# The residual reload of two feed-forward stages: one 4 MB transfer, or eight pieces beside eight output blocks

## The chip, the cores and the metric

The kernel runs on one core of one Trainium2 chip, in one launch. The metric is the device time of that launch in microseconds. A core has a matrix engine (PE), a vector engine (DVE), an activation engine (ACT), GpSimd (POOL) and a queue engine (SP), each with its own instruction stream; they wait for each other on semaphores. Transfers run on 16 DMA engines. Here SP issues the loads of weights (queue q1 in the profile), POOL those of the residual and of the hidden rows (queue q0).

## The reference, cut to what matters

Two blocks of layers on a sequence of 1024 tokens of 1024 channels, in float32. The second block has two feed-forward stages (FFN) with a mixer between them, and each of the three stages adds its normalised result to the stream `x`:

```python
def second_block(x, ...):
    h = rms_norm(x, ffn1_pre_g)
    x = x + 0.5 * rms_norm(swiglu(h, ffn1_w_in, ffn1_w_out), ffn1_post_g)
    h = rms_norm(x, mix_pre_g)
    ...                                   # attention and S5 state space, side by side
    x = x + rms_norm(mixed, mix_post_g)
    h = rms_norm(x, ffn2_pre_g)
    x = x + 0.5 * rms_norm(swiglu(h, ffn2_w_in, ffn2_w_out), ffn2_post_g)
    return x
```

The `x` on the right of each sum is the residual. [...]

## The kernel before, in words

All products are made of float32 operands split in a high and a low part, three products for one. A *block* is one 128-channel column of an output, made from a 128x1024 piece of weights. Its life: SP loads it into `WS` (`load_block`, line 324, two slots in turn); ACT copies it as the high part into `WH` (`split_hi`, line 333), when the block two before has been multiplied; DVE subtracts to get the low part `WL` (`split_lo`, line 340); that frees the `WS` slot, and SP loads the block two further on; PE multiplies (`block_products`, line 376); DVE takes the result out of PSUM. So each engine's order is fixed by hand, and a late load is seen first by ACT, then DVE, then PE.

The second product of an FFN is made in three parts (8, 6 and 8 rows of 128). The third is the *tail*: first the 8 blocks m = 0 to 7 of the first half of the tokens (h = 0), then the same 8 of the second (h = 1), each 24 products of 128x512. In the tail u (u = 1 for the first FFN, 2 for the mixer, 3 for the second FFN), per block: `tail_vector` adds PSUM into `ACC` (line 2205) and then splits the weights of block m + 2, `tail_scalar` copies the high part of block m + 2 and squares the finished column (`post_square`, line 2097), `tail_pool` adds that square to a running sum (`post_sum`, line 2103). At h = 1 the same engines also finish h = 0: `post_apply` scales the column and adds the residual (lines 2129 and 2133), from m = 2 on. The h = 1 half is finished in the next stage's first blocks (`head_vector`) for u = 1, and for u = 3 on PE, where `out_residual` turns the upper half of the residual (line 3601), from m = 2 on.

The residual lies in DRAM as `XRES` (`x_residual` in the profile) and comes back to `RL_X` for u = 1 and 3, which takes the place of `XL`, that is free once the second part's last block has been multiplied. `reload_pool` (line 2299) waits on POOL for that, and issues one transfer of 4 MB. The mixer's tail does it otherwise: `tail_pool` calls `reload_piece` there (line 2305) in the blocks m = 1 to 4 of either half, eight transfers of 512 KB, into `RL_A` and `RL_B`. The semaphore `RESID` counts the reloads (16 for each transfer), and `S5TOE`, a counter of the S5 mixer, is used again for the upper half of the mixer's.

Of the kernel before, what the change touches and what calls it, by code (L numbers as in the profile page):

```python
# [23 lines left out]
KT = D // P  # L24
# [22 lines left out]
S5_T = 8  # L47
# [31 lines left out]
B_MIX = B_FFN1 + FFN_BLOCKS  # L79
# [10 lines left out]
B_END = B_FFN2 + FFN_BLOCKS  # L90
# [54 lines left out]
def _build(nc, ctx, ins, out):  # L145
# [127 lines left out]
    RL_X = at("RL_X", 96, [P, KT, SEQ])  # L273
    RL_A = at("RL_A", 140, [P, 4, SEQ])
    RL_B = at("RL_B", 156, [P, 4, SEQ])
# [22 lines left out]
    XRES = nc.dram_tensor("x_residual", [KT, P, SEQ], F32, kind="Internal").ap()  # L298
# [1765 lines left out]
    FT_TAIL = B_FFN1 + FFN_BLOCKS - 2 * KT  # L2064
    PRE_G = ("f1_pre", "m_pre", "f2_pre")
    POST_G = (None, "f1_post", "m_post", "f2_post")
    RES_COUNT = (0, 16, 80, 96)

    def residual(u, k):
        return RL_X[:, k] if u != 2 else (RL_A[:, k] if k < 4 else RL_B[:, k - 4])  # L2070
# [49 lines left out]
    def post_apply(dve, u, h, rows):  # L2120
        if rows and rows[0] == 0:
            dve.wait_ge(P_RSTD, 2 * (u - 1) + h + 1)
            if h == 0:
                dve.wait_ge(RESID, RES_COUNT[u])
            elif u == 2:
                dve.wait_ge(S5TOE, 16 * S5_T + 64)
        for k in rows:
            x = ACC[:, k, half(h)]
            nc.vector.scalar_tensor_tensor(x, x, vec(POST_G[u], k), RPS[u][:, h], ALU.mult, ALU.mult).then_inc(P_SCALED, 1)  # L2129
        for k in rows:  # L2130
            dve.wait_ge(P_SCALED, place(u - 1, h, k))
            x = ACC[:, k, half(h)]
            nc.vector.tensor_tensor(x, x, residual(u, k)[:, half(h)], ALU.add).then_inc(XRDY, 1)
# [102 lines left out]
    def tail_pool(pool, u):  # L2236
        for h in range(2):
            for m in range(KT):
                if m:
                    post_sum(pool, u, h, m)  # L2240
                if u == 2 and 1 <= m < 5:
                    reload_piece(pool, h, m - 1)
                if h == 1:
                    for k in TAIL_HIGH.get(m, ()) if u < 3 else ():
                        pre_sum(pool, u, 0, k)
        spill_pool(pool, u, 0)
# [49 lines left out]
            pool.wait_ge(XRDY, place(u - 1, h, KT - 1))  # L2296
        pool.dma_start(XRES.rearrange("k p t -> p k t")[:, :, half(h)], ACC[:, :, half(h)]).then_inc(SPILLED, 16)

    def reload_pool(pool, u, b_last):
        pool.wait_ge(SPILLED, 32 * u)  # L2300
        for b in (b_last - 1, b_last):
            pool.wait_ge(BLOCK_DONE[b % 2], times(b))
        pool.dma_start(RL_X[:], XRES.rearrange("k p t -> p k t")).then_inc(RESID, 16)

    def reload_piece(pool, h, n):
        dst, k = (RL_A, RL_B)[n // 2], 2 * (n % 2)
        src = XRES[2 * n:2 * n + 2, :, half(h)].rearrange("k p t -> p k t")
        pool.dma_start(dst[:, k:k + 2, half(h)], src).then_inc(RESID if h == 0 else S5TOE, 16)

# [1043 lines left out]
    def s5_scalar(act, st):  # L3353
        hi = lambda b: split_hi(act, b, cols=cols_of(b))

        def keep_att(m):
            b = att_block(m)
            act.wait_ge(BLOCK_DONE[b % 2], times(b))
            if m == 1:
                act.wait_ge(S5_PRODUCTS, S5STATE[1])  # L3360
            nc.scalar.activation(PARTS[m][:], PS[b % 2][:, half(0)], ACT.Copy).then_inc(PS_READ[b % 2], 1)

        def copy_kernel(k):
            act.wait_ge(S5_PRODUCTS, S5KER[k])
            nc.scalar.activation(s5_half(K0S, k)[0:16], s5_bank(k)[0:16], ACT.Copy).then_inc(S5_COPIES, 1)

        def copy_y(k):
            for r in range(2):
                act.wait_ge(S5_PRODUCTS, S5Yp + 2 * k + r + 1)
                dst = UG[:, 8 * k:8 * k + 8].rearrange("p (q r) m -> p q r m", r=2)[:, :, r]  # L3370
                nc.scalar.activation(dst, s5_bank(r)[:, 4 * (k % 2):4 * (k % 2) + 4], ACT.Copy).then_inc(S5_COPIES, 1)

        def gelu(k):
            act.wait_ge(S5YL[k], YL_BASE[k] + 16)
            nc.scalar.activation(by_place(ZF[:, k]), S5Y[:, k].rearrange("p (j n) -> p n j", j=S5_T), ACT.Gelu_apprx_tanh).then_inc(S5ACT, 1)
            act.wait_ge(S5ACT, 2 * k + 1)
            if k == 0:
                act.wait_ge(S5_RESULTS, 4)
            if k == 3:
                act.wait_ge(S5_PRODUCTS, S5Yp + 8)  # L3380
            nc.scalar.activation(ZH[:, k], ZF[:, k], ACT.Copy).then_inc(S5ACT, 1)

        for k in range(4):
            act.wait_ge(S5_PRODUCTS, S5GT + k + 1)
            nc.scalar.activation(GIN[:, 4 * k:4 * k + 4].rearrange("p q r m -> p (q r m)"), PAB[k % 2][:], ACT.Copy).then_inc(S5_COPIES, 1)
        hi(att_block(2))
        keep_att(0)
        hi(att_block(3))
        copy_kernel(0)
        copy_kernel(1)  # L3390
        hi(att_block(4))
        keep_att(1)
        keep_att(2)
        hi(att_block(5))
        hi(att_block(6))
        copy_kernel(2)
        copy_kernel(3)
        keep_att(3)
        keep_att(4)
        copy_y(0)  # L3400
        copy_y(1)
        hi(B_GLU)
        keep_att(5)
        act.wait_ge(S5TOE, 16 * S5_T)
        gelu(0)
        copy_y(2)
        gelu(1)
        keep_att(6)
        copy_y(3)
        gelu(2)  # L3410
        hi(B_GLU + 1)
        gelu(3)

        def gate(m):
            b = B_GLU + m
            act.wait_ge(BLOCK_DONE[b % 2], times(b))
            if m >= 2:
                act.wait_ge(S5GATED, XLD_END + m - 1)
            nc.scalar.activation(T[m % 2][:], PS[b % 2][:], ACT.Sigmoid, bias=vec("bglu", m)).then_inc(PS_READ[b % 2], 1)
            hi(b + 2)  # L3420

        def gated_high(m):
            act.wait_ge(S5GATED, XLD_END + m + 1)
            nc.scalar.activation(XH[:, m], ZF[:, m], ACT.Copy).then_inc(S5ACT, 1)

        gate(0)
        for m in range(1, 4):
            gate(m)
            gated_high(m - 1)
        gated_high(3)  # L3430
        keep_att(7)
        hi(B_MIXOUT + 1)
        tail_scalar(act, st, 2)
# [76 lines left out]
    def s5_y(pe, k):  # L3510
# [1 line left out]
            pe.wait_ge(S5_COPIES, S5KC + 4)  # L3512
            pe.wait_ge(UD, 16 + 16 * S5_T)
        if k == 2:
            pe.wait_ge(S5TOE, 16 * S5_T)
        if k >= 2:
            pe.wait_ge(S5_COPIES, S5YC + 2 * k - 2)
        pe.wait_ge(S5_RESULTS, k + 1)
# [73 lines left out]

    def out_residual(pe, i):
        if i == 0:
            pe.wait_ge(RESID, RES_COUNT[3])
        if i == 1:
            pe.wait_ge(P_RSTD, 5)
        if i >= 2:
            pe.wait_ge(FCOPY, i - 1)
        for k in range(KT):  # L3600
            last = nc.tensor.transpose(PAB[1 - i % 2][:, k * P:(k + 1) * P], RL_X[:, k, (4 + i) * P:(5 + i) * P], IDENT[:])
        last.then_inc(FTURN, 1)
# [74 lines left out]
    def _(pool):  # L3677
# [5 lines left out]
        ssd_pool(pool)  # L3683
        ln2_pool(pool)
        quads_pool(pool, 0, B_FFN1)
        reload_pool(pool, 1, B_MIX - 2 * KT - 1)
        tail_pool(pool, 1)
        head_pool(pool, 1)
        s5_parameter_loads(pool)
# [5 lines left out]
        tail_pool(pool, 2)  # L3695
        head_pool(pool, 2)
        quads_pool(pool, 1, B_FFN2)
        reload_pool(pool, 3, B_END - 2 * KT - 1)
        out_gains(pool)
        tail_pool(pool, 3)  # L3700

# [63 lines left out]
```

## Time and profile before

| | us |
|---|---|
| median of 3 runs | 3339.81 (3339.54 to 3341.7) |
| the profiled execution | 3333.25 |
| its span (first to last instruction) | 3331.6 |
| PE busy | 3189.6 (96%) |
| DVE busy | 2047.3 (61%) |
| ACT busy | 1301.0 (39%) |
| POOL busy | 376.5 (11%) |
| mean granted PE clock | 0.986 |

The profile is of one execution, shorter than the median of the runs beside it. Times of events are counted from the start of its span. "Idle before" is the time for which an engine stood still just ahead of an instruction, with what released it. Successive products overlap on PE: one of 128x512 is shown 0.39 us long at full clock, and the next begins 0.23 us after it. "PEclk" is the clock that PE was granted, as a share of full speed.

### The profile page before, as it was taken

To read this page: it belongs to the slowest core of one execution; us is meant where nothing else is said; L and a number is where in the kernel's file an instruction comes from. 1 tells how busy PE (TensorE), PEld (TensorE's weight loads), DVE (VectorE), ACT (ScalarE), POOL (GpSimd) and SP (SyncE) were. 2 spreads that over 40 slices of the span, in tenths; PEclk is the share of its full clock that TensorE was granted. 3 is DMA by queue.
4 is the path that set the end of the run, shared out by engine and by line. 5 is a ranking of instruction groups with operands and counts; after the bars stand their busy time and mean duration, and the time that the engine had idled before them with its cause. 6 is when DMAs were issued, how large, how long until landed. Compare 5 with 4: busy or idle time off the path is not lost.

```text
span 3331.6 us, 39702 instructions
## 1 busy us (share of the span) xinstructions
PE 3189.6 (96%) x15786; PEld 2508.4 (75%) x15786; DVE 2047.3 (61%) x2783; ACT 1301.0 (39%) x1924; POOL 376.5 (11%) x412
## 2 busy tenths in 40 slices
PE   8998999999999999899999999998989899999998
PEld 7765677878787786578888877786667678888877
DVE  5545567664554646777777556686665777676334
ACT  2664435452525343742323224314434442323223
POOL 1010000110302010200000003140012300000012
PEclk9999999999999999899999999999999999999999
DMA  6210112222514132332224243422154432225232
GB/s 158 49 42 6 54 51 59 76 83 73 103 51 126 45 94 71 98 112 81 76 96 157 94 141 93 122 70 86 19 119 131 136 98 76 101 76 171 81 115 101
DMA packets 362981, 299.37 MB, mean 90 GB/s; under 512 B 54832, under 2 KB 324624, under 8 KB 362512
## 3 DMA queue, kind: packets, MB, share of 16 engines
q1 hardware_dynamic: 340400, 215.16, 22.6%
q0 software_dynamic: 22400, 81.69, 7.6%
q8 instruction: 126, 2.06, 0.3%
q14 instruction: 55, 0.45, 0.0%
HBM read 240.32 MB, written 52.95 MB: 88 GB/s over the span
## 4 chain that ended last, share of the span: by engine, by line
PE 78%; DVE 10%; ACT 5%; issue 4%; DMA 2%; SPq 0%; POOL 0%; ACTq 0%; DVEq 0%; POOLq 0%
PE PS L376 45%; PE PS L2483 13%; PE PA L2483 7%; PE PS L887 2%; DVE WL L340 1%; PE PA L898 1%; PE PB L1798 1%; DVE XL L2152 1%; DMA WS<-in_ffn_w_out_dram 1%; PE PB L910 1%; PE PA L416 1%; DVE ACC L2129 1%; PE PB L1146 1%; PE PB L1804 1%; PE PA L1780 1%
## 5 line engine op out<-in xcount | busy, mean ns | idle before, releaser
L376 PE MATMUL PS<-XH,WH 128*128 128x512 f32 x1744 | 592.9, 405 | 31.8 <-DVE XL L2152 19.0
L333 ACT ACTIVATE WH<-WS 128x1024 fp32r<-128x1024 f32 (+1 forms) x251 | 242.2, 968 | 846.6 <-PE PS L376 794.1
L376 PE MATMUL PS<-XH,WL 128*128 128x512 f32 x1680 | 554.4, 391 | 0.0
L376 PE MATMUL PS<-XL,WH 128*128 128x512 f32 x1648 | 543.0, 392 | 0.0
L376 PEld LDWEIGHTS PS<-XH,WH 128*128 128x128 f32 x1744 | 326.8, 189 | 127.3 <-DVE XL L2152 27.3
L340 DVE TENSOR_TENSOR WL<-WS,WH 128x1024 fp32r<-128x1024 f32 (+1 forms) x251 | 284.6, 1134 | 167.3 <-ACT WH L333 153.8
L376 PEld LDWEIGHTS PS<-XH,WL 128*128 128x128 f32 x1680 | 317.2, 189 | 67.7
L376 PEld LDWEIGHTS PS<-XL,WH 128*128 128x128 f32 x1648 | 311.3, 189 | 66.2 <-issue 2.2
L376 PE MATMUL PS<-TQH,WH 128*128 128x512 f32 x448 | 162.2, 397 | 7.9 <-DVE WL L340 7.9
L376 PE MATMUL PS<-TQH,WL 128*128 128x512 f32 x448 | 160.5, 393 | 0.0
L376 PE MATMUL PS<-TQL,WH 128*128 128x512 f32 x448 | 160.5, 393 | 0.0
L2483 PE MATMUL PS<-XH,PH 128*128 128x512 f32 x360 | 140.2, 390 | 1.7 <-issue 1.7
L2483 PE MATMUL PS<-XH,PL 128*128 128x512 f32 x360 | 140.1, 389 | 0.0
L2483 PE MATMUL PS<-XL,PH 128*128 128x512 f32 x360 | 140.1, 389 | 0.0
L1911 ACT ACTIVATE DEC<-DEC,NCS 128x128 f32<-128x128 f32 x256 | 78.3, 388 | 98.0 <-POOL DEC L2027 97.9
L1932 DVE TENSOR_TENSOR DEC<-DEC,PB 128x1024 f32<-128x1024 f32 x32 | 39.1, 1222 | 125.6 <-ACT DEC L1911 102.8
L2483 PE MATMUL PS<-TQH,PH 128*128 128x512 f32 x288 | 112.5, 390 | 1.8 <-DVE U3S L2729 1.0
L2483 PE MATMUL PS<-TQL,PH 128*128 128x512 f32 x288 | 112.1, 389 | 0.0
L2483 PE MATMUL PS<-TQH,PL 128*128 128x512 f32 x288 | 112.1, 389 | 0.0
L2483 PE MATMUL PA<-TQH,PH 128*128 128x512 f32 x288 | 112.0, 389 | 0.0
L2483 PE MATMUL PA<-TQL,PH 128*128 128x512 f32 x288 | 112.0, 389 | 0.0
L2483 PE MATMUL PA<-TQH,PL 128*128 128x512 f32 x288 | 112.0, 389 | 0.0
(685 smaller groups left out, 6230.6 us busy)
## 6 DMA issues: line engine op xcount, KB each, us to landing
RAW<-in_ffn_w_in_dram SPq DMA_DIRECT2D x36, 1024.0 KB, 5.2
WS<-in_ffn_w_out_dram SPq DMA_DIRECT2D x48, 512.0 KB, 4.1
WS<-in_ssd_w_in_dram SPq DMA_DIRECT2D x40, 512.0 KB, 3.9
DEC<-ssd_decay_sums SPq DMA_DIRECT2D x32, 512.0 KB, 4.8
WS<-in_ffn_w_in_dram SPq DMA_DIRECT2D x32, 512.0 KB, 4.0
CDX<-ssd_decays SPq DMA_DIRECT2D x56, 256.0 KB, 3.7
TQF<-ffn_hidden POOLq DMA_DIRECT2D x14, 1024.0 KB, 8.2
x_residual<-ACC POOLq DMA_DIRECT2D x6, 2048.0 KB, 7.7
```

The costliest lines, as they stand in the source:

```text
L333: nc.scalar.activation(WH[:, s, 0:cols], WS[:, s, 0:cols], ACT.Copy).then_inc(W_HI[s], 1)
L340: nc.vector.tensor_tensor(WL[:, s, 0:cols], WS[:, s, 0:cols], WH[:, s, 0:cols].bitcast(F32), ALU.subtract).then_inc(W_LO[s], 1)
L376: last = nc.tensor.matmul(PS[s][0:width, c], w[:, s, k * width:(k + 1) * width], x[:, k - x0, c], start=(k == 0 and j == 0), stop=(k == kt ...
L416: last = nc.tensor.matmul(PA[:, h * HALF:(h + 1) * HALF], ONES[:], bufs[k % 2][:, h * HALF:(h + 1) * HALF], start=(k == 0), stop=(k == kts ...
L887: last = nc.tensor.matmul(PS[s][:, a + c * P:a + (c + m) * P], self.queries(p, s)[:, qb * P:(qb + 1) * P], self.keys(p, s)[:, c * P:(c + m ...
L898: last = nc.tensor.transpose(PA[:, s * HALF + (kb - 4 * c) * P:s * HALF + (kb - 4 * c + 1) * P], self.probs(u, s)[:, kb * P:(kb + 1) * P], ...
L910: last = nc.tensor.matmul(PB[HD * s:HD * s + HD, HALF + (qb % 4) * P:HALF + (qb % 4 + 1) * P], self.values(p, s, kb), PT[u % 2][:, s, kb * ...
L1146: last = nc.tensor.matmul(bank, WUQ[:, c // 2, kt], Y[:, 4 + kt, h], start=(kt == 0), stop=(kt == 1))
L1780: nc.tensor.matmul(PA[:, half(c % 2)], BTOK[:, c], XDD[c % 2][:], start=True, stop=True).then_inc(SST, 1)
L1911: last = nc.scalar.activation(d, d, ACT.Exp, bias=NCS[:, c, k:k + 1])
L1932: v.tensor_tensor(DEC[n % 2][:], DEC[n % 2][:], PB[:, 0:P].unsqueeze(1).broadcast_to([P, HPG, P]), ALU.mult).then_inc(SMR, 1)
L2483: last = nc.tensor.matmul(bank, w[:, j, k * P:(k + 1) * P], x[:, k], start=(j in (A11, S2, S1) and k == 0 and t == 0), stop=(k == 3 and t ...
```

## The change: what it does

`reload_pool` becomes `reload_ready`: POOL waits as before, and issues nothing. `tail_pool` issues the pieces for u = 1 and 3 as well: at h = 0, after the sum of block m, piece m (channels 2(m mod 4) and 2(m mod 4) + 1 of 128 each, token half m // 4), so eight pieces of 512 KB in each of the two tails, all in h = 0. Pieces of the lower token half count on `RESID`, those of the upper on `S5TOE`; all waits on these two are moved to the new counts, and two readers of the upper half wait on `S5TOE`: `post_apply` at h = 1 for u = 1, and `out_residual`.

```diff
-    RES_COUNT = (0, 16, 80, 96)
+    RES_COUNT = (0, 64, 128, 192)
+    RES_HIGH = (0, 64, 64 + 16 * S5_T + 64, 64 + 16 * S5_T + 128)
...
             if h == 0:
                 dve.wait_ge(RESID, RES_COUNT[u])
-            elif u == 2:
-                dve.wait_ge(S5TOE, 16 * S5_T + 64)
+            elif u < 3:
+                dve.wait_ge(S5TOE, RES_HIGH[u])
...
                 if u == 2 and 1 <= m < 5:
-                    reload_piece(pool, h, m - 1)
+                    reload_piece(pool, u, h, m - 1)
+                if u != 2 and h == 0:
+                    reload_piece(pool, u, m // 4, m % 4)
...
-    def reload_pool(pool, u, b_last):
+    def reload_ready(pool, u, b_last):
         pool.wait_ge(SPILLED, 32 * u)
         for b in (b_last - 1, b_last):
             pool.wait_ge(BLOCK_DONE[b % 2], times(b))
-        pool.dma_start(RL_X[:], XRES.rearrange("k p t -> p k t")).then_inc(RESID, 16)
-
-    def reload_piece(pool, h, n):
-        dst, k = (RL_A, RL_B)[n // 2], 2 * (n % 2)
+
+    def reload_piece(pool, u, h, n):
+        dst, k = ((RL_A, RL_B)[n // 2], 2 * (n % 2)) if u == 2 else (RL_X, 2 * n)
         src = XRES[2 * n:2 * n + 2, :, half(h)].rearrange("k p t -> p k t")
         pool.dma_start(dst[:, k:k + 2, half(h)], src).then_inc(RESID if h == 0 else S5TOE, 16)
...
-        act.wait_ge(S5TOE, 16 * S5_T)
+        act.wait_ge(S5TOE, 64 + 16 * S5_T)
...
         if k == 2:
-            pe.wait_ge(S5TOE, 16 * S5_T)
+            pe.wait_ge(S5TOE, 64 + 16 * S5_T)
...
     def out_residual(pe, i):
         if i == 0:
-            pe.wait_ge(RESID, RES_COUNT[3])
+            pe.wait_ge(S5TOE, RES_HIGH[3])
...
-        reload_pool(pool, 1, B_MIX - 2 * KT - 1)
+        reload_ready(pool, 1, B_MIX - 2 * KT - 1)
         tail_pool(pool, 1)
...
-        reload_pool(pool, 3, B_END - 2 * KT - 1)
+        reload_ready(pool, 3, B_END - 2 * KT - 1)
         out_gains(pool)
         tail_pool(pool, 3)
```

## Rows read from the trace of the kernel before

**Rows 1.** The page's chain that ended last, by engine.

```profile
PE 78%; DVE 10%; ACT 5%; issue 4%; DMA 2%; SPq 0%; POOL 0%; ACTq 0%; DVEq 0%; POOLq 0%
```

**Rows 2.** The waits of the whole span: us in total, times, longest.

```profile
ACT WH L333 <- DMA WS<-in_ffn_w_out_dram: 20.2, 2, 10.1
```

**Rows 3.** The chain in order of time, first FFN's tail: start, us, what.

```profile
1974.67 14.76 DMA WS<-in_ffn_w_out_dram
...
1989.45 1.06 ACT WH L333
...
1990.54 1.24 DVE WL L340
```

**Rows 4.** The chain in order of time, second FFN's tail.

```profile
3214.84 14.75 DMA WS<-in_ffn_w_out_dram
```

**Rows 5.** PE in order of time, first FFN's tail: start, us, idle before.

```profile
1991.82 0.53 PE L376 MATMUL PS<-TQH,WH 128*128 128x512 f32 x1 [3.27 <-DVE WL L340]
```

**Rows 6.** PE in order of time, second FFN's tail.

```profile
3231.98 0.79 PE L376 MATMUL PS<-TQH,WH 128*128 128x512 f32 x1 [3.27 <-DVE WL L340]
```

**Rows 7.** DVE in order of time, first FFN's tail: results of blocks 1, 3 and 4.

```profile
1983.14 0.69 DVE L2205 TENSOR_TENSOR ACC<-ACC,PS 128x512 f32<-128x512 f32 x1 [3.06 <-PE PS L376]
...
1999.22 0.69 DVE L2205 TENSOR_TENSOR ACC<-ACC,PS 128x512 f32<-128x512 f32 x1 [5.23 <-PE PS L376]
...
2004.66 0.69 DVE L2205 TENSOR_TENSOR ACC<-ACC,PS 128x512 f32<-128x512 f32 x1 [3.06 <-PE PS L376]
```

**Rows 8.** DVE in order of time, second FFN's tail: results of blocks 1 and 3.

```profile
3223.32 0.69 DVE L2205 TENSOR_TENSOR ACC<-ACC,PS 128x512 f32<-128x512 f32 x1 [3.06 <-PE PS L376]
...
3240.59 0.69 DVE L2205 TENSOR_TENSOR ACC<-ACC,PS 128x512 f32<-128x512 f32 x1 [6.44 <-PE PS L376]
```

**Rows 9.** Busy time by stretch: us; PE, PEld, DVE, ACT, POOL; PEclk, DMA share, GB/s.

```profile
1991.80:1999.10 7.30, 7.28 (x25) 5.83 (x26) 2.19 (x2) 0.80 (x2) 3.12 (x2) 0.77 0.48 144
...
3232.00:3240.50 8.50, 8.50 (x25) 6.75 (x26) 2.15 (x2) 0.77 (x2) 3.08 (x2) 0.65 0.45 123
```

**Rows 10.** DMA from 1960 to 2000: packets and MB of each queue; KB each, us to landing.

```profile
q0 software_dynamic: 1040, 4.19, 28.1%
q1 hardware_dynamic: 6112, 3.08, 26.8%
...
RL_X<-x_residual POOLq DMA_DIRECT2D x1, 4096.0 KB, 16.3
```

**Rows 11.** DMA from 1979 to 1982, amid the reload, the same columns.

```profile
q0 software_dynamic: 260, 1.06, 88.4%
q1 hardware_dynamic: 247, 0.13, 14.0%
...
WS<-in_ffn_w_out_dram SPq DMA_DIRECT2D x1, 512.0 KB, 10.8
```

**Rows 12.** DMA from 2562 to 2590, the mixer's tail at h = 1.

```profile
WS<-in_w_mix_out_dram SPq DMA_DIRECT2D x3, 512.0 KB, 4.1
RL_A<-x_residual POOLq DMA_DIRECT2D x2, 512.0 KB, 5.4
```

**Rows 13.** DMA from 2534 to 2546, the mixer's tail at h = 0.

```profile
RL_B<-x_residual POOLq DMA_DIRECT2D x2, 512.0 KB, 6.3
WS<-in_w_mix_out_dram SPq DMA_DIRECT2D x2, 512.0 KB, 6.0
```

**Rows 14.** PE in order of time, the mixer's tail, the first block of h = 1.

```profile
2550.28 0.50 PE L376 MATMUL PS<-XHA,WH 128*128 128x512 f32 x1 [2.02 <-DVE WL L340]
```

**Rows 15.** POOL in order of time, second FFN's tail and the mixer's (last row).

```profile
3264.07 1.80 POOL L2103 TENSOR_TENSOR RP<-RP,SQP 128x512 f32<-128x512 f32 x1 [3.63 <-ACT SQP L2097]
...
2565.91 0.71 POOL L2308 DMA_DIRECT2D RL_A<-x_residual  x1
```

**Rows 16.** The instructions that read RL_X: ns min/median/max, first and last start.

```profile
L2133 DVE TENSOR_TENSOR ACC<-ACC,RL_X x24: 676/679/1781, 2042.9 to 3303.9; 128x512 f32<-128x512 f32 x24
L3601 PEld LDWEIGHTS PB<-IDENT,RL_X x16: 138/140/140, 3279.2 to 3292.7; 128*128 128x128 f32 x16
```

## The prediction

> **What bounds the kernel now.** Read the chain that ended last first: PE holds 78% of it and DMA 2% [rows 1]. The kernel is bound by its products, and a change to a transfer can only pay where a transfer stands in that chain. The list of waits says how much stands in the two FFN: ACT waited twice for a load of output weights, 20.2 us in total [rows 2]. The chain in order of time gives the places: 1974.67 and 3214.84, in the first blocks of the two tails [rows 3, 4]. Each is the load of block 3 of the tail, and each took 14.8 us. The 4 MB reload landed in 16.3 us over the same stretch [rows 10], and amid it, in 3 us, the reload's queue moved 1.06 MB and the weights' queue 0.13 MB; the load of block 4, issued there, took 10.8 us [rows 11]. The packets show why the split is so uneven: the reload's are 4.19 MB / 1040 = 4.0 KB, the weights' 3.08 MB / 6112 = 0.5 KB [rows 10]; with both queues active about as many packets of each went through (260 and 247, rows 11), so the reload takes eight bytes for each one of the weights. The Trainium skill says the same (DMA: Bandwidth & Descriptors, "Queues, rings and completion order"): an engine takes the queues in turn, packet by packet.
>
> What a late load costs is read on PE and in the pace of results. Results of undisturbed blocks leave every 5.44 us (1999.22 to 2004.66, rows 7). Block 3 is issued its load at 1974.67; ACT could take it at the end of block 1, just before 1983.14, so up to 8.3 us to landing cost nothing at all; PE needs it at 1983.0 + 5.44 = 1988.4, and with 1.06 + 1.24 us for the two splits [rows 3] a landing up to 11.4 us after issue costs PE nothing. 14.8 is 3.4 over. PE did stand still for 3.27 us, in both tails [rows 5, 6].
>
> **The change, part by part.** *The 4 MB transfer goes.* First tail: from the result of block 1 to that of block 3 took 1999.22 - 1983.14 = 16.08 us, where two blocks need 10.88: 5.20 us lost [rows 7]. Second tail: 3240.59 - 3223.32 = 17.27, 6.39 lost [rows 8]. That is more than the 3.27 us of standing still, and the stretches show the rest: the block after the stall ran at a mean granted clock of 0.77 and 0.65 of full speed [rows 9], a part of it at 1.2 GHz instead of 2.4. So 6.54 us of standing still and 5.05 us of low clock, 11.59 us together. Both go if no load of the tail takes more than 11.4 us.
>
> *Eight pieces come into the first eight blocks.* No row of the FFN tails shows one, but the mixer's tail has the same piece of 512 KB. At h = 1 there, blocks of 24 products, 512 KB of weights a block and a piece beside it are just what the FFN tails will have: the loads landed in 4.1 us, the pieces in 5.4 [rows 12]. At h = 0 the blocks last half as long, pieces and loads come twice as close, and loads took 6.0 us, pieces 6.3 [rows 13]. A bound from the transfer itself: at 1.06 MB in 3 us [rows 11] a piece of 0.52 MB occupies the engines for 1.5 us, so a load that meets all of it lands in 4.1 + 1.5 = 5.6. I take 4.1 as likeliest and 6.3 as the far end, both under 8.3, so 0 us on the path at either end. Below nothing is excluded, since PE already runs these blocks without a gap outside the stall. Piece 0 leaves right when the last block of the second part is done, with the load of block 3 behind it by 2 us; the 5.6 holds for it too.
>
> *POOL's queue.* Each piece costs 0.71 us of issue; a sum costs 1.8, and POOL stands idle 3.63 us before each sum [rows 15]. 0.71 fits, so no sum moves, among them the last of h = 0 (3264.07 to 3265.9), for which PE waits with the row sum in the first block of h = 1; piece 6 is issued some 3 us before it, piece 7 after it. In the second tail the making of the output gains, 5.5 us, now stands ahead of piece 0 instead of behind the reload; nobody waits for either until h = 1.
>
> *The waits.* DVE needs pieces 0 to 3 for its first residual sum, at 2042.9 in the first tail [rows 16]; the fourth is issued beside block 3 or 4 of h = 0, over 30 us earlier. PE needs pieces 4 to 7 in the second tail at 3279.2 [rows 16]; piece 7 leaves after the sum of block 7, at 3265.9, and lands by 3265.9 + 0.7 + 6.3 = 3272.9, 6 us early. Behind that wait all of PE's last blocks are queued, but it will find the count reached. In the first FFN, DVE's new wait for the upper half stands in the next stage, tens of us later. The moved counts of ACT and PE in the mixer are reached before they are looked at, for the 64 added came in the first tail. All these: 0.
>
> *The price by size of transfer.* One transfer of 4 MB in 16.3 us against eight of 5.4 us, 43 us of landing time, is worse use of the queue [rows 10, 12]. The Trainium skill has this as a rule against the change (DMA: Bandwidth & Descriptors, "Bandwidth"): transfers should be of 1 MiB or more, below that a fixed part of some 2 us tells. By it the pieces would be slower in sum, by seven times 2 us in each tail. Nobody waits for the sum of them here, so I put no term in for it.
>
> **What is late next.** After the stall the tail is bound by PE alone, and at the end of it the chain again goes through PE or through DVE's work behind PE; all of this starts from PE's blocks and moves forward with them. In the second tail the end of the kernel is 90 us away and follows directly. In the first, 5.20 us must be carried through the mixer and the second FFN. I found no row of an event there which comes at a fixed time, but the granted clock after short idle times depends on where they fall, so some of it may be lost or something won.
>
> **The sum.** 5.20 + 6.39 = 11.59 us. The profiled execution would go from 3333.25 to 3321.7 (span 3331.6 to 3320.0). It was 6.56 us under the median of the runs; from the median, 3339.81 - 11.6 = 3328.2.
>
> **The rivals.**
> *A, the first FFN's gain is given back in the mixer* (chance 0.07). The stages between are full of short waits, and one held by something else would take it up. Against it: DMA has 2% of the whole chain. Only 6.39 us remain: 3333.4, at the edge of "the same".
> *B, the low clock comes back elsewhere* (0.06). The stall is gone, but an idle stretch later, moved by some us, is followed by half clock where it wasn't. For it: 0.77 against 0.65 after stalls of the same length [rows 9], so the cost of the clock is no fixed thing. 6.54 us remain: 3333.3.
> *C, the pieces hold up the weights, slower* (0.04). For it: the mixer's tail, where PE waited 2.02 us for a split behind loads of 6 us [rows 13, 14]. If every one of the 16 blocks with a piece paid that, 16 x 2.02 = 32.3, less 11.6, gives 20.7 more: 3360.5. It decides from a landing of 11.4 us on; in the mixer's tail the allowance was half as long, and the worst load took 6.
> *D, the change does not spread the transfer* (0.04). If POOL were behind, it would issue pieces back to back and the weights would be starved as before: 3339.8. Against it: POOL waits before each sum, so each piece is tied to a block's end [rows 15].
> *The forecast*: 0.79.
>
> **How the numbers follow.** A measurement of this kernel can tell about 0.2%, 6.7 us, from no change, so faster is below 3333.1. The forecast lies there almost wholly. Of A and B (3333.4, 3333.3) I count some 0.05 as faster, with half the forecast's own scatter; D is the same; C is slower. Faster 0.84, same 0.12, slower 0.04. The range goes down by one low-clock stretch as in the second tail (6.39 - 3.27 = 3.1), and a little for the runs' scatter: 3324.5. It goes up to A and B and by the 2 us by which the runs before differ: 3335.5.
>
> **What would show it.** In the trace of after: no wait of ACT for a load of output weights in the list; results in both tails 5.44 us apart through blocks 0 to 7, clock 1.00 there; loads of these blocks landing in 4 to 6.3 us, none over 8.3; pieces in 5 to 6.5; POOL idle before each sum about 2.9 us; the first result of h = 1 in the first tail 5.2 us earlier. The stretch from there to the second tail as long as before, within 3 us, would reject A and B. Wrong if loads beside pieces land after 11.4 us, or if the stretch between the tails grows by the gain of the first.

## The result, and the profile after

| | before | after |
|---|---|---|
| median of the runs beside each other, us | 3339.8 (3339.54 to 3341.7) | 3325.25 (3319.76 to 3326.78) |
| after / before, 95% interval | | 0.9947 (0.9935 to 0.9959) |
| the profiled execution, us | 3333.25 | 3326.68 |
| its span, us | 3331.6 | 3324.6 |
| mean granted PE clock | 0.986 | 0.987 |

The changed kernel is faster by 0.53% of 3339.8, 17.7 us by the ratio (the medians lie 14.6 apart). The forecast was 11.6. The same two kernels were run beside each other twice more (below), and gave 0.9966 and 0.9969, 11.4 and 10.4 us; so this first figure is the most favourable of three.

The stalls are gone. In the whole-span list of waits of the changed kernel (us in total, times, longest), ACT's waits for output weights of an FFN have no row any more; where [rows 2] had 20.2 us, ACT now waits for PE alone:

```profile
ACT WH L333 <- PE PS L376: 811.0, 167, 12.5
...
ACT WH L333 <- DMA WS<-in_w_mix_out_dram: 6.7, 3, 3.1
ACT WH L333 <- DMA WS<-in_ab_w_in_dram: 4.2, 1, 4.2
```

The results of the tails leave at an even pace. DVE in order of time, first tail and then second (the lines that answer to [rows 7, 8]; L2206 is L2205 of before):

```profile
1983.21 0.69 DVE L2206 TENSOR_TENSOR ACC<-ACC,PS 128x512 f32<-128x512 f32 x1 [3.06 <-PE PS L376]
1988.65 0.69 DVE L2206 TENSOR_TENSOR ACC<-ACC,PS 128x512 f32<-128x512 f32 x1 [3.06 <-PE PS L376]
1994.09 0.69 DVE L2206 TENSOR_TENSOR ACC<-ACC,PS 128x512 f32<-128x512 f32 x1 [3.06 <-PE PS L376]
...
3222.68 0.69 DVE L2206 TENSOR_TENSOR ACC<-ACC,PS 128x512 f32<-128x512 f32 x1 [3.06 <-PE PS L376]
3228.12 0.69 DVE L2206 TENSOR_TENSOR ACC<-ACC,PS 128x512 f32<-128x512 f32 x1 [3.06 <-PE PS L376]
3233.56 0.69 DVE L2206 TENSOR_TENSOR ACC<-ACC,PS 128x512 f32<-128x512 f32 x1 [3.06 <-PE PS L376]
```

Every distance is 5.44 us, where [rows 7] had 16.08 for two blocks and [rows 8] 17.27. Busy time by stretch (us; PE busy and products, PEclk, DMA share, GB/s) shows no idle time and no low clock in either:

```profile
1978.00:1994.00 16.00, 16.00 (x72) 1.00 0.48 141
...
3217.00:3234.00 17.00, 17.00 (x76) 1.00 0.56 166
```

The DMA view from 1980 to 2024, seven of the pieces amid the loads (against [rows 10]):

```profile
q1 hardware_dynamic: 8320, 4.19, 32.3%
q0 software_dynamic: 1008, 3.67, 26.6%
...
WS<-in_ffn_w_out_dram SPq DMA_DIRECT2D x9, 512.0 KB, 4.2
RL_X<-x_residual POOLq DMA_DIRECT2D x7, 512.0 KB, 5.0
```

The packets are as large as before (3.67 MB / 1008 = 3.6 KB, 4.19 MB / 8320 = 0.5 KB), but a load meets 0.5 MB of the residual instead of 4. The load of block 3 landed in 5.6 us, the next in 4.2, and none of the tail took over 5.7.

**Where the time went in the pair of profiles.** The same instruction of both kernels, at four places: a result of block 3 in the first tail is 5.13 us earlier; a DVE row of the next stage (`MK<-PS,T`) is 7.64 us earlier; one behind the mixer (`T<-PS,T`) is only 0.60 us earlier; the end is 7.02 earlier. Before, then after:

```profile
2115.03 0.68 DVE L2900 TENSOR_TENSOR MK<-PS,T 128x512 f32<-128x512 f32 x1
...
2697.36 0.68 DVE L2669 TENSOR_TENSOR T<-PS,T 128x512 f32<-128x512 f32 x1
```

```profile
2107.39 0.68 DVE L2902 TENSOR_TENSOR MK<-PS,T 128x512 f32<-128x512 f32 x1
...
2696.76 0.68 DVE L2671 TENSOR_TENSOR T<-PS,T 128x512 f32<-128x512 f32 x1
```

Read alone, this pair says that rival A or B came true: 5.2 us won in the first tail, 2.5 more in the next stage, and 7.0 given back in the mixer. That is the first thing which the experiments had to settle.

### The profile page after: what moved, and what is told of

It reads as the page before. It is cut to its first block, busy times and chain, and to the rows that moved or that the text cites. A ratio compares the mean times of both kernels' runs of the same rounds, so it can differ in the third digit from the quotient of the medians.

```text
span 3324.6 us, 39717 instructions
## 1 busy us (share of the span) xinstructions
PE 3183.2 (96%) x15786; PEld 2505.3 (75%) x15786; DVE 2045.7 (62%) x2783; ACT 1300.9 (39%) x1924; POOL 382.2 (11%) x426
## 4 chain that ended last, share of the span: by engine, by line
PE 79%; DVE 10%; ACT 5%; issue 4%; DMA 1%; SPq 0%; POOL 0%; ACTq 0%; DVEq 0%; POOLq 0%
PE PS L376 46%; PE PS L2485 13%; PE PA L2485 7%; PE PS L887 2%; DVE WL L340 1%; PE PA L898 1%; PE PB L1798 1%; DVE XL L2153 1%; PE PB L910 1%; PE PA L416 1%; DVE ACC L2130 1%; PE PB L1146 1%; PE PB L1804 1%; PE PA L1780 1%; PE PS L1511 1%
## 5 line engine op out<-in xcount | busy, mean ns | idle before, releaser
L376 PE MATMUL PS<-XH,WH 128*128 128x512 f32 x1744 | 592.4, 404 | 31.6 <-DVE XL L2153 18.2
```

The costliest lines, as they stand in the source:

```text
L376: last = nc.tensor.matmul(PS[s][0:width, c], w[:, s, k * width:(k + 1) * width], x[:, k - x0, c], start=(k == 0 and j == 0), stop=(k == kt ...
```

## The experiments

Theory: the whole gain is that of the two stalls, and they come from the large packets of the 4 MB transfer, which starve the loads. Rivals: the mixer gives the first gain back (A or B of the prediction); the pieces still cost something; the gain is partly another.

To compare executions, each kernel's DVE instructions were put beside those of the profiled execution of before, and the difference in time read at the ends of four stretches: the stall in the first tail (1983.1 to 1999.2), the rest of that tail and the next stage (to 2115.0), the mixer (to 2700), and the stall in the second tail (3223.3 to 3240.6). Positive is longer than in that execution, in us:

| kernel | first stall | to 2115 | mixer | second stall |
|---|---|---|---|---|
| before, again (e0) | +1.11 | +0.06 | +7.85 | +0.02 |
| spill later (e9) | -0.04 | -1.72 | +5.94 | -1.41 |
| only second tail (e3) | -0.19 | +0.02 | +7.48 | -6.39 |
| only first tail (e2) | -5.20 | -1.73 | +5.28 | -1.52 |
| after | -5.20 | -2.51 | +7.04 | -6.39 |
| changed, again (e1) | -5.20 | -2.55 | +4.50 | -6.39 |
| changed, third time (e10) | -5.21 | -2.52 | +8.69 | -6.39 |
| two halves (e5) | -5.19 | -1.73 | +9.04 | -6.39 |
| mixer's piece later (e11) | -5.20 | -2.55 | +7.57 | -6.39 |
| all at once (e4) | +0.92 | -1.73 | +5.04 | +0.43 |
| no reload (e7) | -5.20 | -0.78 | -0.73 | -6.39 |
| wide weights (e8) | -5.20 | -0.80 | +5.12 | -6.43 |

In e2 and e9, 1.4 us more than in the profile of before come between the second stall and the end, and in e8 4.2 us. They lie in PE's last products, some 80 us behind the stall: the granted clock from 3320 to 3325 is 0.66 in e2, and 0.50 in e8, where it is 1.00 before. e8 has no stall in the second tail, so this low clock is not the stall's, put off. e6 is not in the table, since its stall falls on other blocks.

The table leaves out the start of the kernel up to 1983.1, the same code in all of them. It too differs: beside the profile of before it took 0.1 us longer in that of after, 1.8 in e0 and e3, 3.8 in e1, 5.7 in e10. The profiled execution of before was the shortest of all there.

### The kernel before, against itself

No edit.

> The kernel before, unchanged, timed against itself. Theory (each tail loses a stall and its low clock, 5.2 and 6.4 us, the rest is scatter of the stages between): a ratio of 1.000, single times between 3333 and 3342 us, and in its trace the load of block 3 in both tails near 14.8 us and PE standing still 3.3 us again. Rival (the profiled execution of before, 6.6 us under its median, shows stages that the usual execution does not): the trace of a usual execution of 3340 us has more half-clock stretches or longer waits between the two tails (2040 to 3212 us), by 6 us in sum.

Measured 3343.51 (3336.56 to 3345.96, 11 runs) beside 3341.65 (3336.61 to 3350.21, 24 runs), ratio 0.9999 (0.9989 to 1.0009). The stall is there again (PE idle 3.12 and 3.21 us, the load of block 3 in 14.6). But its mixer took 7.85 us longer than that of the profile of before. So the mixer's length differs between executions of one kernel, and the profiled execution of before was a lucky one there. Of the 10.8 us between the two profiled executions 7.85 lie in the mixer, 1.8 ahead of the first tail and 1.1 in its stall; the 6.56 us by which the first lay under its median are most likely of the same kind. The place is the S5 part, where PE waits for a load of the driving input. PE in order of time, before:

```profile
2423.13 0.44 PE L3491 MATMUL PA<-UG,GIN 128*64 128x128 f32 x4 [2.28 <-DMA UG<-s_u]
```

and after:

```profile
2418.30 0.69 PE L3493 MATMUL PA<-UG,GIN 128*64 128x128 f32 x4 [6.04 <-DMA UG<-s_u]
```

After the longer idle time the products take 0.69 instead of 0.44 us, and from 2426 to 2446 the granted clock is 0.91 against 1.00. The unchanged code in e0 waited 4.8 us at the same line, and its clock from 2426 to 2446 was 0.91 as well; the changed kernel waited 3.9 us in e1 and 6.75 in e10. So the long wait needs no change to come.

### The changed kernel, twice more

No edit to the changed kernel.

> The changed kernel, unchanged, on another chip session. Theory: 11.6 us less than before, ratio 0.9965, with a scatter of some 3 us that comes from the mixer. Rival (the change gains more than the two stalls, as the first measurement's 0.9947 says): 14 to 18 us less again, ratio 0.995, and in the trace the stretch between the tails is shorter than in a usual execution of before by 3 to 6 us.

Measured 3331.09 (3327.91 to 3334.91, 6 runs), ratio 0.9966 (0.9954 to 0.9978).

> The changed kernel a third time, for its size. By the traces so far: first tail 5.2 to 6.3 us, second tail 6.4, the stage after the first tail 1.7 to 2.5, together 13.3 to 15.2 us, ratio 0.9955 to 0.9960. If only the two stalls count: 11.6 us, 0.9965.

Measured 3331.67 (3327.01 to 3335.94, 10 runs) beside 3342.9 (20 runs), ratio 0.9969 (0.996 to 0.9979). The three ratios, weighted by their intervals, give 0.9962, 12.7 us. The intervals of the first (0.9935 to 0.9959) and the third (0.996 to 0.9979) don't meet, so sets of runs differ by more than an interval says, and 12.7 us is uncertain by some 4 us (an estimate from how far the three lie apart). The mixer took 4.5 and 8.7 us more than in the profile of before, e0, e3 and e9 with the unchanged code around it 7.9, 7.5 and 5.9: no loss that goes with the change can be seen.

### One tail alone

Only the first tail in pieces; the second has the whole transfer:

```diff
-                if u != 2 and h == 0:
+                if u == 1 and h == 0:
...
+    def reload_whole(pool):
+        pool.dma_start(RL_X[:], XRES.rearrange("k p t -> p k t")).then_inc(RESID, 16)
```

> Eight pieces in the first FFN's tail only; the second FFN reloads in one transfer as before. Theory: 5.2 us less than before (ratio 0.9984), stall of 3.3 us left in the second tail. Rival (what is gained beyond the stalls comes from the mixer, which starts at another moment): 8 to 12 us less, ratio 0.997, the surplus lying between 2040 and 3212 us.

Measured 3334.55 (3331.88 to 3336.98), ratio 0.997 (0.9958 to 0.9981), some 10 us. One wait of ACT for an output weight is left:

```profile
ACT WH L333 <- DMA WS<-in_ffn_w_out_dram: 10.0, 1, 10.0
```

Only the second tail in pieces (`if u == 3 and h == 0`, `reload_whole` ahead of the first):

> Eight pieces in the second FFN's tail only. Theory: 6.4 us less than before (ratio 0.9981), since all after it is PE's work and moves with it; scatter as that of before. Rival (surplus from the mixer): the same 5 to 6.5 us here, because nothing before the second tail has moved, so that first-only and second-only differ by the surplus.

Measured 3336.13 (3332.22 to 3345.88), ratio 0.9981 (0.9971 to 0.9991), 6.3 us, as the 6.39 of the second stall. Each part pays by itself, and the first tail's gain reaches the end of the kernel, which rivals A and B deny. It is not smaller than the second's but, by these runs, larger than the 5.2 us of its stall; the stretch to 2115 is shorter by 1.73 in e2, and unchanged in e3. The two gains add up to some 16 us, where the whole change gained 11.4 beside the same runs of before; the intervals allow both, so the times alone can't divide the gain.

### Spreading, not cutting

The eight pieces issued one behind the other, where the 4 MB transfer stood:

```diff
-                if u != 2 and h == 0:
-                    reload_piece(pool, u, m // 4, m % 4)
...
+    def reload_burst(pool, u):
+        for m in range(8):
+            reload_piece(pool, u, m // 4, m % 4)
```

> The same eight pieces with the same waits, but all issued one after the other where the 4 MB transfer stood, none beside a block. Theory (what starves the weights is 4 MB standing in the queue at once, whatever its cut): the load of block 3 takes 13 to 15 us, PE stands still 2 to 3.5 us in each tail and its clock falls again; 8 or more of the gained 11 to 14 us are lost, ratio to before 0.999 to 1.001. Rival (small transfers as such let the weights through): that load lands under 11.4 us, PE doesn't stop, ratio 0.996 as the changed kernel.

Measured 3341.3 (3336.8 to 3343.08), ratio 0.9998 (0.9989 to 1.0008): no gain. The stalls are there, a little longer. Waits, and PE in the first tail (against [rows 2, 5]):

```profile
ACT WH L333 <- DMA WS<-in_ffn_w_out_dram: 21.9, 2, 11.1
```

```profile
1997.01 0.50 PE L376 MATMUL PS<-TQH,WH 128*128 128x512 f32 x1 [4.22 <-DVE WL L340]
```

So it is the spreading over the blocks that pays, and the size of a transfer by itself does nothing. This is what rival D would have looked like.

### Two halves

Two transfers of 2 MB, beside blocks 0 and 4:

```diff
-                if u != 2 and h == 0:
-                    reload_piece(pool, u, m // 4, m % 4)
+                if u != 2 and h == 0 and m in (0, 4):
+                    reload_half(pool, m // 4)
```

> Two transfers of 2 MB in each FFN tail, ahead of block 1 and after block 4's sum, in place of eight pieces. Theory (a load is late by the time the reload's bytes occupy the engines, 2.1 MB at 1.06 MB in 3 us = 5.9 us, and PE notices from a landing of 11.4 us on): the load of block 3 lands after 9 to 11 us, the one beside the second half too, ACT waits some 1 to 2 us for it, PE doesn't stop, time as that of the changed kernel, ratio 0.996. Rival (any landing over 8.3 us, where ACT begins to wait, costs): PE stands still 1 us or more in each tail and with the clock half of the gain is lost, ratio 0.998.

Measured 3327.01 (3323.6 to 3330.62, 4 runs), ratio 0.9952 (0.9934 to 0.997), as fast as eight pieces. The load of block 3 took 9.8 us, over the 8.3 that ACT allows and under the 11.4 that PE allows: ACT waited 5.1 us at most, and the results still left every 5.44 us. The two allowances of the prediction, read from the profile of before, hold; half the volume is little enough.

### No reload at all

The FFN tails transfer nothing. The residual sum adds the column to itself, and the last products of the output turn a constant tile instead of the residual, so the output is another:

```diff
-                if u != 2 and h == 0:
-                    reload_piece(pool, u, m // 4, m % 4)
```

> The changed kernel without any reload in the two FFN tails; the sum adds the scaled column to itself in place of the residual, and PE turns a constant tile where it turned the residual, so the instructions are as many and as long. Theory (the pieces are hidden wholly): the same time as the changed kernel within its scatter of 3 us, tails with blocks of 5.44 us as there, ratio to before 0.9955 to 0.997. Rival (the pieces still cost something, in DVE or POOL or through the weights): 2 us or more below the changed kernel, and blocks of the tails that are shorter than there.

Measured 3325.28 (3322.68 to 3327.77, 4 runs), ratio 0.9949 (0.9932 to 0.9965). This interval overlaps that of each of the three comparisons of the changed kernel, the last (0.996 to 0.9979) by little. In the trace the tails are alike to 0.01 us: -5.20 and -6.39 in both. Within the tails the pieces cost nothing. The rest of the difference from 0.9962 may lie in the mixer, which in e7's profile was 0.73 us shorter than that of the profile of before, where the others' were 4.5 to 9 longer; whether that comes from the missing transfers or is chance, one profile can't tell.

### Why the loads were starved: the size of the packets

The reload of before, read in runs of 512 bytes (so the residual's values come in another order, and the output is another):

```diff
-        pool.dma_start(RL_X[:], XRES.rearrange("k p t -> p k t")).then_inc(RESID, 16)
+        src = XRES.rearrange("k p (a c) -> p a k c", a=KT)
+        pool.dma_start(RL_X[:].rearrange("p a (k c) -> p a k c", k=KT), src).then_inc(RESID, 16)
```

> The kernel before with its one transfer of 4 MB, read in runs of 512 bytes instead of 4 KB; the channels of the residual arrive in another order in the FFNs, so their sums are made with the wrong elements, of the same number. Theory (engines share by packets, and the reload's packets are eight times as large as the weights'): with packets of one size the load of block 3 gets half of the engines and lands in 8 to 10 us, PE doesn't stop in the tails, the reload takes 20 us or more, ratio 0.996 to 0.998. Rival (the weights come late because their queue stands behind, whatever the packets): 14 us or more and the 3.3 us stall stay, or worse as the reload lasts longer, ratio 1.000 or above.

Measured 3348.84 (3342.33 to 3353.89), ratio 1.0019 (1.0007 to 1.0031). The edit missed its aim. DMA from 1976 to 2012:

```profile
q0 software_dynamic: 1040, 4.19, 40.3%
q1 hardware_dynamic: 5200, 2.62, 27.0%
...
RL_X<-x_residual POOLq DMA_DIRECT2D x1, 4096.0 KB, 24.0
```

The shorter runs were put into as many packets as before, 1040 of 4 KB, and only the transfer became slower (24.0 against 16.3 us, [rows 10]). So the packets' size was not varied. What it does show: the stall grows with the time for which the large packets are in the way (PE idle 5.99 and 5.62 us; the loads of blocks 4 and 5 took 17.5 and 13.5).

So the size was varied on the other side, in before: the weights of the tails read in runs of 4 KB, which are the wrong weights, with the reload whole and at its place:

```diff
+                if n == 2:
+                    src = w_out[(m % KT) * P:(m % KT + 1) * P, :].rearrange("p (k c) -> p k c", k=KT)
```

> The kernel before with its 4 MB transfer, but the weights of both FFN tails are read as 4 KB rows of the matrix instead of 512-byte pieces of rows; the products use the wrong weights of the same number. Theory (packets of the two queues pass one for one, so bytes are shared by packet size): with packets of one size the load of block 3 has half of the engines, 0.52 MB at half of 0.35 MB per us = 3 us, and lands in 5 to 7 us instead of 14.8, though the whole reload is queued; PE doesn't stop, both tails keep 5.44 us a block, ratio to before 0.995 to 0.997. Rival (a load issued behind a reload waits for it, whatever its packets): 12 us or more, the stall stays, ratio 1.000.

Measured 3328.24 (3323.67 to 3334.45, 4 runs), ratio 0.9959 (0.9943 to 0.9975): as large a gain as the change's, within the intervals, with nothing spread. DMA from 1965 to 2010:

```profile
q0 software_dynamic: 1040, 4.19, 24.3%
q1 hardware_dynamic: 1075, 3.88, 23.4%
...
RL_X<-x_residual POOLq DMA_DIRECT2D x1, 4096.0 KB, 18.2
```

The loads are now 3.88 MB / 1075 = 3.6 KB a packet, as large as the reload's. The load of block 3 took 8.0 us against 14.8, the next 7.4, and PE did not stand still. The reload took 18.2 us instead of 16.3. With equal packets, and both queues active, the two share evenly, in packets and in bytes. DMA from 1988 to 1990 in e8:

```profile
q0 software_dynamic: 103, 0.42, 51.5%
q1 hardware_dynamic: 100, 0.41, 50.1%
```

With packets of an eighth the load waited for nearly all of the reload. The prediction took from the Trainium skill (DMA: Bandwidth & Descriptors, "Queues, rings and completion order") that an engine takes the queues in turn by packet; these counts agree. One part of the delay has nothing to do with the packets' size: the first packet of the load of block 3 starts 3.8 us after its issue in before and 3.5 in e8, where it is 1.0 for a load with nothing beside it (e7). Some 2.5 of the 3.9 us by which e8's load is late are this; with the reload in pieces it is 1.5 us (after). Why the first packet is late is open.

### The 2.5 us that no term foresaw

Between the two stages, DVE makes pairs of `XL<-ACC,VT,XH`, and POOL puts the residual out (the spill) and then goes on with a sum, `T<-T,SQQ`. Before, in order of time:

```profile
2111.96 3.15 DVE L2152 SCALAR_TENSOR_TENSOR XL<-ACC,VT,XH 128x512 fp32r<-128x512 f32 x2
2112.33 0.92 POOL L2297 DMA_DIRECT2D x_residual<-ACC  x1 [8.30 <-DVE ACC L2133]
...
2112.62 2.48 DVE L2152 SCALAR_TENSOR_TENSOR XL<-ACC,VT,XH 128x512 fp32r<-128x512 f32 x1
2113.27 1.28 POOL L2160 TENSOR_TENSOR T<-T,SQQ 128x512 f32<-128x512 f32 x1
```

and after:

```profile
2106.07 1.40 DVE L2153 SCALAR_TENSOR_TENSOR XL<-ACC,VT,XH 128x512 fp32r<-128x512 f32 x2
2106.78 0.91 POOL L2300 DMA_DIRECT2D x_residual<-ACC  x1 [8.64 <-DVE ACC L2134]
2107.71 1.30 POOL L2161 TENSOR_TENSOR T<-T,SQQ 128x512 f32<-128x512 f32 x1
```

The pair before this one takes 1.40 us in both kernels, but this one, where POOL's issue began 0.37 us after the pair's start, took 3.15 before: its second instruction, begun 0.29 us behind the issue, lasted 2.48 us. The DVE rows behind it come 1.75 us later. After the change POOL stood idle 8.64 instead of 8.30 us behind the same releaser, began 0.71 us after the pair's start, and the pair took 1.40. How long DVE is held up goes by the sum, and not by the issue ahead of it. An undisturbed instruction of the kind lasts 0.74 us. The lengthened one ended at 2115.10, 0.55 us behind the sum's end (2114.55). After, the second ran from 2106.73 to 2107.47, and the sum began at 2107.71. The same 0.55 us stand behind other lengthened ones; the next pair of before, beside a later sum:

```profile
2116.39 2.06 POOL L2160 TENSOR_TENSOR T<-T,SQQ 128x512 f32<-128x512 f32 x1
2117.25 1.75 DVE L2152 SCALAR_TENSOR_TENSOR XL<-ACC,VT,XH 128x512 fp32r<-128x512 f32 x1
```

All 43 instructions of the three kinds `XL<-ACC,VT,XH`, `ACC<-ACC,VT,RP` and `ACC<-ACC,VT,T` that last over 1 us in before end 0.55 or 0.56 us behind the end of a POOL sum. One that starts amid an issue with no sum near behind it keeps its length:

```profile
1374.57 0.94 POOL L2297 DMA_DIRECT2D x_residual<-ACC  x1
1375.10 0.74 DVE L1452 SCALAR_TENSOR_TENSOR ACC<-ACC,VT,T 128x512 f32<-128x512 f32 x1
```

Which of the two engines gives way is not settled by this: an instruction of DVE at 2577.33, 0.53 us into an issue with a sum right behind it, kept its 0.74 us. The spill behind the mixer's tail meets DVE in the same way (2.49 us at 2651.19), and still does after the change (2.47 at 2652.01).

The experiment gave POOL of the kernel before some waits that are already met, ahead of this spill:

```diff
+                for _ in range(8):
+                    pool.wait_ge(SPILLED, 32)
```

> The kernel before, with eight waits that are already met ahead of the spill that POOL issues in the stage after each of the first two tails, so that the spill and the sum behind it start some 0.3 us or more later. Theory (in six kernels that spill starts 0.34 us later than in the four others, and in just these six DVE's operation beside it takes 0.7 instead of 2.4 us): DVE's pair of low parts (line 2152) takes 1.4 instead of 3.15 us here too, the stretch from 2040 to 2115 us is 1.5 to 2 us shorter than in the kernel before, while both tail stalls stay. Rival (that stretch is shorter only where the first tail's transfer was changed): 3.15 us again, no change of the stretch.

Measured 3340.85 (3336.98 to 3342.73, 8 runs), ratio 0.9998 (0.9987 to 1.0009). Both stalls are there (PE idle 3.27 and 3.26 us), and the rows of the pair read as after the change:

```profile
2114.93 1.40 DVE L2152 SCALAR_TENSOR_TENSOR XL<-ACC,VT,XH 128x512 fp32r<-128x512 f32 x2
2115.58 0.92 POOL L2300 DMA_DIRECT2D x_residual<-ACC  x1 [8.58 <-DVE ACC L2133]
2116.52 1.29 POOL L2160 TENSOR_TENSOR T<-T,SQQ 128x512 f32<-128x512 f32 x1
```

The second instruction ran from 2115.59 to 2116.33, and the sum began at 2116.52. The stretch to 2115 is 1.72 us shorter, so it hangs on when POOL's spill and sum start, and not on the stall or the residual. The edit moved spill and sum together; that the sum sets the length is read from the rows above. The time of the whole shows nothing of it: 1.7 us is within the interval. The Trainium skill (SBUF — State Buffer, "Who interferes with whom") says that a DVE instruction with two inputs in on-chip memory contends with a GpSimd instruction that reads it; the sum is one, and the 0.55 us in these rows agree. It also says that who issues first decides. Of 42 instructions of the three kinds that start during a sum in before, 41 are lengthened, which agrees; the one here starts 0.65 us ahead of the sum (2112.62, 2113.27) and is held up all the same, so its start alone doesn't tell it. Open stays why POOL is 0.3 us later in the changed kernel. It stood idle 8.64 us in every kernel that issues parts in the first tail (after, e1, e2, e4, e5, e10, e11), and 8.30 in before, e0, e3, e7 and e8, which have the whole transfer there or none; but in e6, which has the whole one, it was 8.60.

The other 0.8 us of the 2.5 are a low clock that did not come. Both kernels have the same idle time of PE here, 2.40 and 2.41 us, and then the same products. Before, row and stretch:

```profile
2077.44 0.78 PE L376 MATMUL PS<-XH,WH 128*128 128x512 f32 x1 [2.40 <-DVE XL L2152]
...
2077.40:2082.40 5.00, 4.96 (x11) 0.66 0.80 276
```

and after:

```profile
2072.33 0.50 PE L376 MATMUL PS<-XH,WH 128*128 128x512 f32 x1 [2.41 <-DVE XL L2153]
...
2072.30:2077.30 5.00, 4.97 (x18) 1.00 0.81 278
```

With 0.66 the stretch lies between the two levels, 1.2 GHz for a part of it, with 1.00 it is at 2.4 GHz throughout. The column "to 2115" of the table is these two events: -1.7 alone where only the spill is later (e2, e4, e5, e9), -0.8 alone where only the low clock is missing (e7, e8), -2.5 where both are so (the changed kernel three times, and e11), nothing in before, e0 and e3. The stall alone doesn't decide on the clock: e5 has no stall and still has the low clock. What does is open.

### The mixer's pieces, one later

The mixer's tail has the same pieces in blocks half as long, and PE still waits there for a split ([rows 13, 14]; 2.02 us again after the change). Rival C put that on the piece. Here the fourth piece of h = 0 is issued behind block 7 instead of block 4:

```diff
-                if u == 2 and 1 <= m < 5:
-                    reload_piece(pool, u, h, m - 1)
+                if u == 2 and (1 <= m < 4 or m == (7 if h == 0 else 4)):
+                    reload_piece(pool, u, h, min(m - 1, 3))
```

> The changed kernel, and in the mixer's tail the last of the four pieces of the lower half is issued after the sum of block 7 instead of block 4, so that it doesn't meet the first 512 KB loads of weights. Theory (a piece delays a load by the 1.5 us that its bytes take, and only here, at 2.7 us a block, PE notices): the loads that took 6 us land in 4.5 to 5.5, PE stands still 0.5 to 1 us instead of 1.5 to 2.0 us ahead of the first block of h = 1, 1 to 1.5 us less in all, which the times can't tell: ratio to before as the changed kernel's, 0.995 to 0.997. Rival (the loads themselves, 512 KB in blocks of half the length, make that wait): 1.5 to 2 us of standing still remain.

Measured 3329.39 (3325.57 to 3331.04, 7 runs) beside 3339.38 (11 runs), ratio 0.9967 (0.9955 to 0.9978), as the changed kernel in its second and third comparison. The loads took 6.1 and 4.2 us (after: 6.3 and 5.8), and PE still waited:

```profile
2552.14 0.50 PE L376 MATMUL PS<-XHA,WH 128*128 128x512 f32 x1 [1.69 <-DVE WL L340]
```

1.69 us lies within the 1.46 to 2.02 of the three profiles of the changed kernel. So the piece is not what PE waits for there; the first of the two loads still met an earlier piece and took 6.1, so a load free of all pieces was not seen, and the expected gain was not either. None of the runs beats the changed kernel.

## Why the prediction was right or wrong

- **What bounds the kernel, and the mechanism: right.** One large transfer with large packets starved two loads (the 3.8 us before the first packet, which the prediction did not see, are a part of it); the chain and the list of waits had named both. Spreading takes it away (e4 against after), and so do equal packets (e8).
- **The allowances of 8.3 and 11.4 us: right.** At 9.8 ACT waits and PE does not (e5); at 14.6 and more PE does (e0, e4).
- **The stalls' terms, 5.20 and 6.39: right for the execution they came from.** In the changed kernel both come off to 0.01 us. Over four executions with the first stall (before, e0, e3, e9) it cost 5.20, 6.31, 5.01 and 5.16, 5.42 in the mean: the idle time stays at 3.1 to 3.3, the low clock behind it varies. In the second tail it cost 6.39 in before, 6.41 in e0, 4.87 in e2 and 4.98 in e9, 5.66 in the mean.
- **The pieces at nothing: right.** Loads 4.1 to 5.7 us where 4.1 was taken and within the 6.3 of the far end; pieces 4.1 to 5.9, median 5.0, a little faster than the 5.4 of [rows 12]. Without any transfer the tails end at the same moment (e7). POOL's idle time before a sum was to be 2.9:

```profile
1986.68 0.72 POOL L2310 DMA_DIRECT2D RL_X<-x_residual  x1
1990.37 1.79 POOL L2104 TENSOR_TENSOR RP<-RP,SQP 128x512 f32<-128x512 f32 x1 [2.97 <-ACT SQP L2098]
```

- **"POOL's queue" at nothing: this step failed.** It looked for what POOL does in the tail, where no sum moved, and not for what POOL meets when it comes 0.3 us later to the next stage: DVE's instruction is no longer held up until the sum is done. That is worth 1.75 us there, and another 0.8 of a low clock stayed away: 2.5 us in each trace of the changed kernel (and in e11). The sum by these traces is 5.4 + 2.5 + 5.7 = 13.6 us, and 14.1 with the two stalls as in the profile of before, where the prediction said 11.59. The times can't tell which: the three intervals are 13.7 to 21.7, 7.4 to 15.4 and 7.0 to 13.4 us, their weighted mean 12.7.
- **The Trainium skill's rule for transfers of 1 MiB or more** (DMA: Bandwidth & Descriptors, "Bandwidth") speaks against the pieces and changes nothing in the time: nobody waits for their sum. Two halves of 2 MB keep to it and are as fast (e5), so obeying it costs nothing either.
- **Rivals A and B: rejected, though the first pair of profiles looks like them.** The stretch between the tails is 4.5 us longer in that pair (-2.51 + 7.04), more than the 3 us that I had given as proof against my forecast. It was the wrong test: the profiled execution of before is itself 7.9 us shorter in the mixer than a second execution of the same code. The prediction had the sign of this before it, the 6.56 us between the profiled execution and the median, and did not ask where they lay.
- **Rivals C and D: rejected** by the tails' even pace; D's picture is that of e4.
- **The range: too narrow.** 3324.5 to 3335.5 holds the median of 3325.25 by 0.75 us, but the first ratio puts the kernel at 3322.1. The failed step is "a little for the runs' scatter": it was given 0.6 us at the low end (3328.2 - 3.1 - 3324.5) and 2 us at the high one, from three runs. Over all comparisons the kernel before ran from 3333.0 to 3350.2, the mixer alone moves by up to 9 us from one execution to the next, and the code ahead of the first tail by up to 5.7. That the second and third comparison (0.9966 and 0.9969) lie within 1.2 us of the 11.59 is in part luck: 2.5 us that no term had stand in their traces too.

## What to carry to other kernels

When a load is late beside another transfer, compare bytes per packet of the two queues: while both are active they share by packets, so the one with small packets gets little, and the cure is to spread the large one over several blocks (two parts were enough here) or to make the small packets large. Work out how late a load may land before PE notices, from the pace of results, and size the parts by that. Where the profiled execution lies well off the median, find the stretch that makes it so before two profiles are compared, for one pair can show a loss that no code made.

## What the hardware showed that was not expected

- The same code took 7.9 us longer in one stage of one execution than of another: a wait for a load at PE of 2.3 or 4.8 us (3.9, 6.0 and 6.75 with the change). From 2426 to 2446, behind it, the granted clock was 1.00 after 2.3 us and 0.91 after 4.8 and 6.0, 1.2 GHz for a part of it.
- A DVE instruction with two inputs in on-chip memory that is held up beside a POOL sum ends 0.55 us behind that sum: 2.48 us instead of 0.74 at 2112.62. Amid a DMA issue of POOL with no sum near it, one kept its 0.74 (1375.10). A third of a microsecond on POOL, which is busy for 11% of the span, so moves the stages behind by 1.7 us.
- The first packet of a load of weights starts 1.0 us after its issue with nothing beside it (e7), and 3.8 or 3.5 us after it behind a fresh 4 MB reload (before, e8).
- A source read in runs of 512 bytes on POOL's queue still went in packets of 4 KB (1040 for 4.19 MB), and took 24.0 us instead of 16.3. On SP's queue the packets had 0.5 KB.
- After an idle time of PE of 2.40 us the granted clock was 0.66 over the next 5 us in one kernel and 1.00 in another after 2.41 us, with the same products behind it.
